# The running sum of squares of three normalisations kept by GpSimd instead of VectorE

## The reference, cut to what matters

```python
def rms_norm(x, w):
    xf = x.astype(jnp.float32)
    y = xf * lax.rsqrt(jnp.mean(xf * xf, axis=-1, keepdims=True) + EPS)
    return (y * w.astype(jnp.float32)).astype(x.dtype)

def modulate(x, w, shift, scale):
    return rms_norm(x, w) * (1 + scale[:, None, :]) + shift[:, None, :]
...
x = x + y_mixer * gate            # after each stage
...
return rms_norm_2(x_lat, final_g)
```

## Time and profile before

| | |
|---|---|
| median of 3 runs | 2469.42 (2467.05 to 2469.99) |
| profiled execution, its time | 2468.88 |
| profiled execution, its span | 2467.2 |
| TensorE matmul busy | 2388.7 (97%) |
| VectorE busy | 1477.5 (60%) |
| ScalarE busy | 964.6 (39%) |
| GpSimd busy | 384.8 (16%) |
| adds into acc | 42, median 0.692 each |

### The profile page before, as it was taken

One profiled execution on the slowest core, in us unless ns is written; L12 is line 12 of the kernel. 1 busy time (PEld: TensorE's weight loads), 2 busy tenths in 40 slices (PEclk: granted clock), 3 DMA queues, 4 the chain that ended last, 5 costly groups with the idle time before them and its releaser, 6 DMA issues. The chain is left out here.

```text
span 2467.2 us, 33317 instructions
## 1 busy us (share of the span) xinstructions
PE 2388.7 (97%) x12140; PEld 1985.5 (80%) x12140; DVE 1477.5 (60%) x1946; ACT 964.6 (39%) x1522; POOL 384.8 (16%) x499
## 2 busy tenths in 40 slices
PE   5999999999999999999999999999999998999997
PEld 4788887666787788887888888888888886788886
DVE  6766544765445766634665666666666666655555
ACT  4333322634433333333444454444444444423223
POOL 0111000000000111000143343333333332000000
PEclk8999999999999999999999999999999999999999
DMA  6666532211223666533211111111111111222221
GB/s 266 231 222 219 186 137 91 80 65 52 69 91 115 216 220 210 176 112 105 69 58 55 46 49 61 52 61 60 61 58 54 52 50 53 82 70 78 74 77 43
DMA packets 69564, 254.39 MB, mean 103 GB/s; under 512 B 7632, under 2 KB 7760, under 8 KB 69456
## 3 DMA queue, kind: packets, MB, share of 16 engines
q1 hardware_dynamic: 51312, 186.82, 22.4%
q0 software_dynamic: 18144, 66.07, 7.8%
HBM read 250.76 MB, written 2.10 MB: 102 GB/s over the span
## 5 line engine op out<-in xcount | busy, mean ns | idle before, releaser
L198 PE MATMUL ps<-hH,wh 128*128 128x512 f32 x1776 | 711.2, 400 | 5.1 <-DVE wl L194 2.3
L200 PE MATMUL ps<-hH,wl 128*128 128x512 f32 x1776 | 693.7, 391 | 0.0
L199 PE MATMUL ps<-hL,wh 128*128 128x512 f32 x1776 | 692.6, 390 | 0.0
L194 DVE TENSOR_TENSOR wl<-raw,wh 128x1024 fp32r<-128x1024 f32 x331 | 411.0, 1242 | 402.0 <-ACT wh L189 398.9
L189 ACT ACTIVATE wh<-raw 128x1024 fp32r<-128x1024 f32 x331 | 348.2, 1052 | 272.9 <-PE ps L200 192.4
L198 PEld LDWEIGHTS ps<-hH,wh 128*128 128x128 f32 x1776 | 334.2, 188 | 76.9 <-issue 11.3
L200 PEld LDWEIGHTS ps<-hH,wl 128*128 128x128 f32 x1776 | 333.6, 188 | 71.5
L199 PEld LDWEIGHTS ps<-hL,wh 128*128 128x128 f32 x1776 | 334.4, 188 | 68.4 <-issue 3.8
L1863 POOL TENSOR_TENSOR XR<-XR,fp 128x512 f32<-128x512 f32 x112 | 143.0, 1277 | 572.1 <-ACT KQ L1561 572.1
L523 POOL DMA_DIRECT2D araw<-in_ada x120 | 63.6, 530 | 874.7 <-ACT rs L254 367.3
L1689 DVE TENSOR_TENSOR XL<-XL,fp 128x512 f32<-128x512 f32 x112 | 134.7, 1202 | 9.2 <-ACT KQ L1561 9.2
(11 more groups left out here) (323 smaller groups left out, 3741.1 us busy)
## 6 DMA issues: line engine op xcount, KB each, us to landing
raw<-in_ws SPq DMA_DIRECT2D x331, 512.0 KB, 3.5
araw<-in_ada POOLq DMA_DIRECT2D x120, 512.0 KB, 5.0
praw<-in_ada SPq DMA_DIRECT2D x16, 512.0 KB, 10.4
xin<-in_x SPq DMA_DIRECT2D x1, 2048.0 KB, 9.0
out_x<-xout SPq DMA_DIRECT2D x1, 2048.0 KB, 6.4
cin<-in_ctx POOLq DMA_DIRECT2D x1, 1024.0 KB, 5.2
traw<-in_dfts POOLq DMA_DIRECT2D x2, 512.0 KB, 4.0
cst<-in_const SPq DMA_DIRECT2D x1, 512.0 KB, 3.3
```

The lines of the kernel that those rows point to most:

```text
L194: dve.tensor_tensor(wl[:, j, :], raw[:, j, :], wh[:, j, :].bitcast(F32), ALU.subtract).then_inc(lo_ready, 1)
L198: pe.matmul(o, a_hi, b_hi, start=start, stop=False, **kw)
L199: pe.matmul(o, a_hi, b_lo, start=False, stop=False, **kw)
L200: return pe.matmul(o, a_lo, b_hi, start=False, stop=stop, **kw)
```

## The change

The adds of the norms 0, 4 and 5 are taken off VectorE's list and put on GpSimd's: seven right behind its first memset, seven between the recurrence mixer and the table loads, seven at the end. `acc_add` itself keeps its two waits and its instruction. The clearing of acc stays on VectorE, and so do the adds of the norms 1, 2 and 3.

```diff
-        def acc_add(dve, m, k, n=T):
-            dve.wait_ge(sq_done, 8 * m + k + 1)
-            dve.wait_ge(acc_step, 8 * m + k + 1)
-            dve.tensor_tensor(acc[:, 0:n], acc[:, 0:n], sq[:, 0:n], ALU.add).then_inc(acc_step, 1)
+        def acc_add(eng, m, k, n=T):
+            eng.wait_ge(sq_done, 8 * m + k + 1)
+            eng.wait_ge(acc_step, 8 * m + k + 1)
+            eng.tensor_tensor(acc[:, 0:n], acc[:, 0:n], sq[:, 0:n], ALU.add).then_inc(acc_step, 1)
...
                 out_dve(dve, HG_OUT + 8 + o, o, o)
-                if o:
-                    acc_add(dve, 4, o - 1)
...
-        def ft_out_dve(dve, g, total=False):
+        def ft_out_dve(dve, g):
...
-                if total and o:
-                    acc_add(dve, 5, o - 1)
...
-            ft_out_dve(dve, last, total=True)
+            ft_out_dve(dve, last)
...
         @block.gpsimd
         def _(pool):
             pool.memset(epsc[:, :], EPS).then_inc(setup, 1)
+            for k in range(KD - 1):
+                acc_add(pool, 0, k)
             pool.wait_ge(s_cact, 1)
             pool.wait_ge(rs_step, 2)
...
             hg_pool(pool)
+            for k in range(KD - 1):
+                acc_add(pool, 4, k)
             ft_pool(pool)
+            for k in range(KD - 1):
+                acc_add(pool, 5, k)
...
                                              pacc[:, u // 8, :], ALU.mult, ALU.add).then_inc(s_pacc, 1)
-                if u < KD - 1:
-                    acc_add(dve, 0, u)
                 if u == 11:
                     collect_dve(dve, 0, 0)
```

## The result

The changed kernel takes 2480.75 us (median of 5, 2479.70 to 2482.31) against 2469.42 before: +11.3, ratio 1.0049 with a 95% interval of 1.0035 to 1.0064. The direction and the likeliest case were as forecast; the loss is 1.65 times the forecast 6.9, near the upper end of the range. The profiled execution of the changed kernel took 2480.75 at a span of 2479.1.

A forecast was written before the change was run, and what follows sets the result against it. TensorE, busy 97% of the span, was taken as the bound, VectorE mattering only where TensorE waits for it. Terms 1.8 + 1.8 + 1.65 + 1.6 = +6.85 on 2469.4 gave 2476.3, range 2471.5 to 2481.5.

The forecast's parts named there:

- the likeliest case: Whole kernel: turns at SBUF in the opening and a fallen clock at the end; 2476.3, range 2473.5 to 2481, chance 0.55.
- Only the three waits matter: Relieving VectorE counts only where TensorE waits for it, in the stretches before three normalisations: opening, Fourier mixer, closing norm.
- The price of an add: 1.05: Each GpSimd add was priced at 1.05 from its product of the same size, bounds 0.9 to 1.3.
- Hand-overs: Square chains: ScalarE to GpSimd takes 0.08, the way back 0.10, up to 0.25 for the bound.
- Turns at SBUF in the opening: Opening: pacc products and GpSimd adds take turns, period 2.07 against 1.80, chain end +1.8, bounds 0 to +5.0.
- Hold and lock: Opening: an add holds VectorE for 0.79; the skill's stronger whole-instruction lock, 1.05, would cost some 1.8 more.
- Rival (4): Opening: every add holds VectorE for its own length or 1.32; in all +8.7 to +10, about 2478.8, chance 0.10.
- (1): Turns at SBUF in the opening and a fallen clock at the end; 2476.3, chance 0.55.
- The load pins the opening: Opening: the 12th product still starts at 29.61 behind its load, so faster early products gain 0.
- Fourier input: Norm before the Fourier mixer: square period 1.86, seventh add ends 1.8 later, bounds +0.8 to +4.1.
- Table loads: Behind the adds before the Fourier mixer: three loads on GpSimd's queue move by some 2, at cost 0.
- Closing norm: Kernel's end: seventh add +1.65, TensorE's idle wait 1.7 to 3.35, then +1.6 from norm passes at 1.2 GHz.

The follow-up runs named there:

- add_forms: Changed kernel with norm 4's GpSimd adds taking a second operand of 8 elements repeated 64 times, and norm 5's seven made products; one execution, 2478.30 us.
- warm_close: Changed kernel with 19 idle matmuls keeping TensorE busy in the wait before the closing norm; 2477.69 us, ratio 1.0039.

## Where the prediction held, and the step that failed

- **Only the three waits matter.** Right. The pieces between them are the same to 0.1, and the three places make up the whole.
- **The price of an add: 1.05.** This is the step that failed. It measured 1.26 to 1.29. The row it was taken from was a product of the same size, but with a repeated second operand; with such an operand the add is 1.04. The error of 0.2 stands seven times in each square chain: the period came out at 2.06 to 2.10 and not at 1.86. That makes the whole of the 1.4 that was missing at norm 4 (+3.2 where I had +1.8), as add_forms shows (13.0 where 13.2 was forecast), and the 1.1 at norm 5 (+2.8 where I had +1.65). The bound of 1.3 that I kept held it.
- **Hand-overs.** Right: ScalarE to GpSimd 0.08 (2091.10 to 2091.18), the way back 0.10 (2092.47 to 2092.57).
- **Turns at SBUF in the opening.** The mechanism is right; the sum of 1.8 was not, the chain lost 2.8. I had built the period as a hold of 0.79 and a product of 1.28. The hold measured 0.82, but a product stands 1.39 behind the one before even when nobody holds it, 0.10 of it between the two; my own rows showed that (5.45 for four). So the period is 2.21 and not 2.07, and six times 0.14 is 0.8 of the 1.0 that was missing. The same 0.10 is in the 0.28 of waiting that I took to go whole. That the hold came out so near is luck: an add of 1.05 would by the turns measured here (all but 0.14 of it, then 1.08) give a period of 1.99, an estimate from those rows. Its longer length made up for that.
- **Hold and lock.** The Trainium skill (SBUF — State Buffer, "SBUF: two separate sides") has the two engines exclude each other for a whole instruction. The trace agrees, but for the first 0.14 of the add and the first 0.20 of the product. I had read that rule as a hold of the add's full length, and my 0.79 as something milder. They are the same thing: the held product's own first 0.20 and the 0.10 in front of it pass meanwhile, so a turn of 1.12 delays it by 0.82. Rival (4), with holds of the full length, is out, although the measured time is nearer to its 2478.8 than to the 2476.3 of (1).
- **The load pins the opening.** Right, and the sharpest point: no adds at all give 17.35 to the 12th product, as before.
- **Fourier input.** The split's place in VectorE's queue did cost the old chain 1.3: its adds start 1.45 apart, and 2.75 where the split stands between them (2092.02 to 2094.77). The chain of the changed kernel is as worked out, with the add put in at its real length: 6 x 2.07 + 0.71 + 1.26, and 0.14 for the meeting with the split, is 14.5; it measured 14.6. Table loads: no cost, as forecast.
- **Closing norm.** The wait grew to 4.9, not 3.35. From the second square (2447.08) to the end of the seventh add it is 12.4 where I had 11.1, which is the 0.2 an add once more. The passes ran at 1.2 GHz as forecast, all four of them (+1.7), and some closing transposes too (+0.8): 2.5 where I had taken 1.6. This second miss is not the add's price: I had put a part of the passes ahead of the fall and given the transposes only some chance. warm_close gives the 2.5 back.
- **Sum.** 1.8, 1.8, 1.65, 1.6 were forecast, 2.8, 3.2, 2.8, 2.5 measured. Each is inside its own bounds and all are off to the same side. The wrong price alone makes the two square chains' part of it, and it went into the opening as well; I had treated the four as independent terms, which left the range little room at the top.

## What to carry to other kernels

Before moving small work to an idle engine, ask whether the engine it leaves is ever late. Here the opening waited for a load and the two later chains for a single buffer. The adds on VectorE cost nothing in the first; at norm 4 a second buffer with the adds left on VectorE brought the norm matmul 1.3 earlier (10.11 instead of 11.39), where GpSimd brought it 3.2 later. And price an instruction from a row with the same operands, not only with the same shape: a length that enters a serial chain seven times needs it, and its error goes into several terms at once.

## What the runs showed of the hardware that I had not expected

- GpSimd's two-input operation on 128 x 512 float32 took 1.26 to 1.29 with two whole operands, sum or product alike, and 1.04 with a second operand of 8 elements repeated 64 times.
- GpSimd's adds and VectorE's instructions with two SBUF operands took strict turns. A VectorE instruction on 1024 columns ended 1.07 to 1.09 behind the end of the add before it, whether product or weight split, and an add of 512 columns ended 1.12 behind the end of that instruction; one of 256 columns 0.58.
- So a product was held for 0.82 by a 1.27 add and for 0.28 by one of 0.73: in both 0.45 less than the add takes alone.
- A held instruction's recorded length depends on when it starts against the other's: the weight split took 1.45 when it met the end of an add, and 2.22 when it met one at its start, each time for a single turn of GpSimd.
